# Causal mask of an attention stage: added on VectorE in PSUM in place of a TensorE product with the identity

## The reference

```python
def block(args):
    qb, cb, s0 = args
    s = jnp.einsum('bhqd,bhkd->bhqk', qb, kh).astype(f32) * scale
    s = s + cb[..., None] - c[:, :, None, :]
    q_pos = s0 + jnp.arange(Q_BLOCK, dtype=jnp.int32)
    mask = k_pos[None, :] <= q_pos[:, None]
    p = jax.nn.softmax(jnp.where(mask, s, -jnp.inf), axis=-1)
    return jnp.einsum('bhqk,bhkd->bhqd', p.astype(vh.dtype), vh)
```

## Time and profile before

| | us |
|---|---|
| median of 3 runs | 2705.4 |
| the 3 runs | 2704.35, 2705.4, 2709.52 |
| the profiled execution | 2702.63 |
| its span, first to last instruction | 2700.8 |
| PE busy in it | 2632.7 (97%) |
| DVE busy | 1499.2 (56%) |
| ACT busy | 1115.2 (41%) |
| POOL busy | 882.5 (33%) |
| mean granted clock of TensorE | 0.989 |

### The profile page before, as it was taken

How to read it: one execution, slowest core, us unless ns; L and a number is a source line. 1 busy time by engine, 2 the same in 40 slices (tenths; PEclk the granted TensorE clock), 3 DMA queues, 4 the chain that set the end, 5 groups by cost and what they waited for, 6 DMA issues and landing times.

```text
span 2700.8 us, 34562 instructions
## 1 busy us (share of the span) xinstructions
PE 2632.7 (97%) x13990; PEld 2201.0 (81%) x13990; DVE 1499.2 (56%) x1688; ACT 1115.2 (41%) x1301; POOL 882.5 (33%) x201
## 2 busy tenths in 40 slices
PE   7989889999899999999999999999999999999998
PEld 6866778888798988888888888898988888888887
DVE  3674646999763383354674346734473364645435
ACT  4364535778534442334332223434433343422222
POOL 2211020000132344444444443433343454344444
PEclk9999988999999999999999999999999999999999
DMA  3330024999221373223233333321662232333332
GB/s 135 118 134 17 1 100 165 367 372 371 76 94 63 126 290 130 78 101 125 101 108 125 119 116 117 106 79 63 233 220 94 94 117 94 109 117 118 120 129 109
DMA packets 61300, 361.26 MB, mean 134 GB/s; under 512 B 7280, under 2 KB 8176, under 8 KB 26096
## 3 DMA queue, kind: packets, MB, share of 16 engines
q1 hardware_dynamic: 58720, 353.49, 35.7%
q10 hardware_dynamic: 2448, 5.90, 0.6%
HBM read 357.25 MB, written 2.10 MB: 133 GB/s over the span
## 4 chain that ended last, share of the span: by engine, by line
PE 80%; DVE 4%; ACT 1%; issue 1%; ACTq 0%; DVEq 0%
PE pd L270 19%; PE pd L272 19%; PE pd L271 19%; PE pd L291 2%; PE pd L290 2%; PE pd L289 2%; PE pd L2142 2%; PE pd L2144 2%; PE pd L2143 2%; DVE sb_y_lo L1874 2%; DVE sb_h_lo L543 1%; PE pd L2169 1%; PE pd L2171 1%; PE pd L2170 1%; PE pd L2099 1%
## 5 line engine op out<-in xcount | busy, mean ns | idle before, releaser
L224 POOL TENSOR_TENSOR sb_w_lo<-sb_raw,sb_w_hi 128x2048 fp32r<-128x2048 f32 x181 | 845.4, 4671 | 1715.7 <-ACT sb_w_hi L215 1715.7
L270 PE MATMUL pd<-sb_h_hi,sb_w_hi 128*128 128x512 f32 x1600 | 635.7, 397 | 11.4 <-DVE sb_h_lo L543 5.1
L272 PE MATMUL pd<-sb_h_hi,sb_w_lo 128*128 128x512 f32 x1600 | 625.2, 391 | 0.0
L271 PE MATMUL pd<-sb_h_lo,sb_w_hi 128*128 128x512 f32 x1600 | 625.0, 391 | 0.0
L215 ACT CAST sb_w_hi<-sb_raw 128x2048 fp32r<-128x2048 f32 x185 | 353.6, 1912 | 349.8 <-PE pd L272 324.3
L270 PE MATMUL pd<-sb_y_hi,sb_w_hi 128*128 128x512 f32 x960 | 376.2, 392 | 8.0 <-DVE sb_y_lo L1885 3.9
L272 PE MATMUL pd<-sb_y_hi,sb_w_lo 128*128 128x512 f32 x960 | 374.1, 390 | 0.0
L271 PE MATMUL pd<-sb_y_lo,sb_w_hi 128*128 128x512 f32 x960 | 374.1, 390 | 0.0
L270 PEld LDWEIGHTS pd<-sb_h_hi,sb_w_hi 128*128 128x128 f32 x1600 | 301.6, 189 | 80.5 <-issue 6.8
L272 PEld LDWEIGHTS pd<-sb_h_hi,sb_w_lo 128*128 128x128 f32 x1600 | 301.5, 188 | 63.8
L271 PEld LDWEIGHTS pd<-sb_h_lo,sb_w_hi 128*128 128x128 f32 x1600 | 301.8, 189 | 62.4 <-issue 1.9
(11 more groups left out here) (568 smaller groups left out, 3837.4 us busy)
## 6 DMA issues: line engine op xcount, KB each, us to landing
sb_raw<-in_slabs SPq DMA_DIRECT2D x190, 1024.0 KB, 4.7
sb_moe_raw<-in_moe SPq DMA_DIRECT2D x56, 1024.0 KB, 5.0
sb_raw<-in_moe SPq DMA_DIRECT2D x28, 1024.0 KB, 4.8
sb_QK<-in_ada SPq DMA_DIRECT2D x32, 512.0 KB, 5.2
sb_V<-in_ada SPq DMA_DIRECT2D x32, 512.0 KB, 5.5
sb_M<-in_ada SPq DMA_DIRECT2D x16, 512.0 KB, 3.6
sb_Y<-in_ada SPq DMA_DIRECT2D x16, 512.0 KB, 5.5
sb_MG<-in_ada SPq DMA_DIRECT2D x16, 512.0 KB, 5.6
```

The costliest lines, as they stand in the source:

```text
L224: pool.tensor_tensor(w_lo[j][:], raw[j][:], w_hi[j][:].bitcast(F32), ALU.subtract).then_inc(w_lo_ready[j], 1)
L270: pe.matmul(out, w_hi[j][:, cols], hi[:, k], start=(k == 0), stop=False)
L271: pe.matmul(out, w_hi[j][:, cols], lo[:, k], start=False, stop=False)
L272: last = pe.matmul(out, w_lo[j][:, cols], hi[:, k], start=False, stop=(k == KT - 1))
```

## The change

The second product of scores(n) is taken out, and the first one closes the accumulation and raises sc_done. VectorE, once sc_done is there, adds maskneg to the last 128 columns of the same PSUM bank, in place, waits for that to end (through v) and then takes the maximum as before.

```diff
-                          start=True, stop=False)
-                pe.matmul(out[:, keys - P:keys], ident[:], maskneg, start=False, stop=True).then_inc(sc_done, 1)
+                          start=True, stop=True).then_inc(sc_done, 1)
...
                     dve.wait_ge(sc_done, n + 1)
                     if n >= 4:
                         dve.wait_ge(sc_exp, n - 3)
+                    last = pd[n % 2][:, keys - P:keys]
+                    v(dve.tensor_tensor(last, last, maskneg, ALU.add))
                     v(dve.tensor_reduce(small[:, 32 + n % 4:33 + n % 4], pd[n % 2][:, 0:keys], AX.X, ALU.max,
                                         negate=True), sc_max, n + 1)
```

## The result

| | before | changed |
|---|---|---|
| median | 2705.3 us (20 runs) | 2717.5 us (20 runs) |
| profiled execution | 2702.63 us | 2722.2 us |
| its span | 2700.8 us | 2720.4 us |
| its granted clock | 0.989 | 0.979 |

The changed kernel takes 1.0048 times the time of the kernel before (95% interval 1.0034 to 1.0061), by this ratio 13 us more. The forecast was 2709.0 us (+3.6) with a range up to 2715. Two of the 20 runs of the changed kernel lie far outside the rest, at 3768.9 us (mean clock 0.65) and 13337.6 us (1.00); why is not known, the ratio and all that follows leave them out, and the median of the other 18 is 2717.0 us.

What follows compares the result with a forecast made beforehand. The prediction took a loop through TensorE, VectorE and ScalarE to bound the score units. Additions of 6.27 us, less 1.53 us of products and 1.16 us of idle time, gave +3.6 us on 2705.4: 2709.0 us, range 2702 to 2715.

Steps and rivals of the forecast that it cites:

- one more stretch at the half clock: Rival, slower: wider TensorE gaps bring one or two more 3 us half-clock stretches, 2710.5 to 2712 us; chance 0.10.
- The price of the addition: Each VectorE mask addition in the score units: 0.29 us plus 0.04 wait, 0.33 us (bounds 0.20 and 0.73).
- The expensive write to PSUM: Rival, slower: VectorE's addition writing to PSUM takes 0.42 us plus 0.04, +6.1 us, 2711.5 us; chance 0.12.
- Units 4 to 7: Score units with VectorE's queue unbroken: TensorE's saving brings nothing, four additions cost 4 x 0.33 = +1.32 us.
- latency sum: Over the score units: 19 additions, 6.27 us, less 1.53 us of products and 1.16 us of idle time: +3.6 us.
- units that I gave to VectorE's queue or to ScalarE: Score units such as 4 to 7 (VectorE) or 8, 9, 22, 23 (ScalarE), where TensorE's saving was counted as nothing.
- Units 0 to 3 at nothing: Beside the recurrence: product hidden beneath VectorE's work, addition fits in 0.62 us idle; cost nothing, without cover 1.3 us.
- The exponential's wait: Sign in the score units: ScalarE's wait for the maximum grows from 36.4 us, by about 0.1 us a unit or more.
- VectorE's wait for TensorE: Sign in the score units: the maximum's wait for the mask product, 13.2 us, passes to the addition and shrinks.
- TensorE decides everywhere: Rival, faster: additions hide in VectorE's idle time, each unit gives back its product, 7.0 us, 2698.4 us; chance 0.06.
- every addition counts: Rival, slower: all 32 additions on the path, TensorE's saving never, 10.6 us, 2716.0 us; chance 0.12.
- The slower sign: Whole kernel slower by over 0.2%, above 2710.8 us; chance 0.32, summed from rivals and the forecast's own tail.

Runs made afterwards that it cites:

- neither: The kernel before without the mask product on TensorE and without the addition on VectorE, so with no causal mask: 2707.7 us, ratio 1.0027.
- again: The changed kernel run once more, unaltered: 2718.3 us (5 runs), ratio 1.0068 to the kernel before.
- the kernel with the four kept products: The changed kernel with the mask product kept in units 0 to 3 and filler products ahead of the transposes from unit 4 on: 2708.1 us, ratio 1.0028.
- the early mask product: The kernel before with the mask product issued first in its accumulation, one iteration sooner: ratio 1.0004; with the 12 fillers added 2701.5 us, ratio 0.9999.

## Why the prediction was wrong

**The part that failed is the rival that I called one more stretch at the half clock.** I gave it a chance of 0.10 and one or two stretches of 3 us, 1.5 us each. The changed kernel's mean clock is 0.0061 below that of the kernel before. Over 2717 us this is about 33 us more at the half clock, where the rival had three or six. Its price, 0.5 us for each, was not far off: the changed kernel's two profiles gave 0.36 us, and the slopes of 1.78 to 2.55 us for 0.001 of the mean clock make 0.0061 worth 11 to 16 us, against a measured loss of 13. So the mechanism was on the list, and its size was wrong by a factor of five or more. Two steps led there. I priced the removed product by its time on the path alone, so a product beneath a wait had the price zero; "neither" shows that removing all 32 of them, with nothing added, makes the kernel slower by 0.27% while its level falls by 3.4 us. And I took the two half-clock stretches of one profile as fixed, where the runs of the kernel before spread from 0.984 to 0.991 of mean clock. The page that I cited beside that rival (the Trainium skill, TensorE: Matmul & The Clock Gate, on oscillation) names this mechanism, gaps in the matmul stream that bring the 1.2 GHz level back, and the traces agree: behind a stretch in which PE was busy 0.30 of 3 us the clock fell to 0.62, and with that stretch filled it stayed at 1.00.

**The price of the addition was right.** 300 ns measured, 285 to 290 taken; with its wait 0.33 us (the rows below: 0.34 from start to start). The expensive write to PSUM, a rival with 0.12, did not happen. Of the two estimates that I had from the Trainium skill (VectorE: DVE Perf Modes, TRN2 errata), 0.291 us is 3% short of the measured 0.300, and 0.258 us 14%. In the changed kernel's units 4 and 5, at the full clock:

```profile
292.09 0.30 DVE L1676 TENSOR_TENSOR pd<-pd,sb_c 128x128 f32<-128x128 f32 x1
...
292.43 0.69 DVE L1677 TENSOR_REDUCE sb_small<-pd 128x1 f32<-128x512 f32 x1
...
295.60 0.30 DVE L1676 TENSOR_TENSOR pd<-pd,sb_c 128x128 f32<-128x128 f32 x1
...
304.93 0.69 ACT L1370 ACTIVATE sb_H<-pd,sb_small 128x512 f32<-128x512 f32 x1 [3.03 <-DVE sb_small L1677]
```

**Units 4 to 7: right.** From the maximum of unit 4 (292.43) to the exponential of unit 7 (304.93) it took 12.50 us; before it was 286.75 to 298.25, 11.50. Three additions lie between, 3 x 0.33 = 1.0. The stretch ran at the full clock.

**The rest of the latency sum: the right sign of each term, in total too large or just right.** It had +5.1 us for the additions and -1.5 for the products. The levels give +4.5 and -3.4, the lines at 0.988 +4.5 and -2.8. The removed product was worth about twice what I gave it: I counted 6 of the 32 on the path, and 2.8 to 3.4 us at 0.22 is 13 to 15. In units that I gave to VectorE's queue or to ScalarE, TensorE's saving seems to have arrived all the same; which units these are was not resolved. For the whole change the levels give zero (2699.8 and 2699.0 against 2699.7), the lines +2.2 us at 0.988, the profiles about 1.5. The predicted +3.6 us is at the upper end of this and is neither confirmed nor refuted.

**Units 0 to 3 at nothing: right by latency.** The kernel with only these four units changed has the level 2699.5 and a ratio of 1.0008 that can't be told from 1.

**What the prediction said it would show.** The exponential's wait grew, as said. VectorE's wait for TensorE grew in the first profile (17.9 against 13.2 us) and shrank, as said, in that of "again" (9.5 us), which had less half clock; so the growth was the sign that time was lost by TensorE's clock. The transposes I had wrongly put 0.22 us behind their old place relative to the score passes: without the product they come sooner, in unit 5 0.92 us after the score product's start ("again", 286.82 to 287.74) and not 1.13 (287.06 to 288.19). Of the gap after the last maximum I had said that it stays as it was: it was 10.8 us before (353.71 to 364.50) and is 11.1 us (370.03 to 381.16).

**The other rivals.** That TensorE decides everywhere (faster) and that every addition counts were both refuted by the comparisons at an equal clock, which lie between them. The slower sign had 0.32 in all; the mechanism that decided had only 0.05 of that, half of its own 0.10.

**What stays open.** Shown is that removing the product lowers the granted clock, that keeping it holds the clock, and that the loss of time follows the clock. Not settled is why nearly as many products elsewhere (30 fillers) win back only about half of it (0.9849 and 0.9853 against 0.9878); the kernel with the four kept products is too near to both to tell. Also open is why units 0 to 3 run at the half clock in some executions of the changed kernel (the first profile) and not in others ("again").

## What to carry to other kernels

In a stage where TensorE waits for other engines all the time, price a removed TensorE operation twice: by its time on the path, and by what the granted clock does afterwards; the second can be several times the first and of the other sign. Before trusting a latency sum of a few microseconds, set each run's time against its mean granted clock, and compare kernels at an equal clock: that splits latency from clock with runs that one has anyway. Do it at a clock that both kernels reached: the slope of time over clock was 2.55 us for one of these kernels and 1.78 for the other, and a common slope hides a few microseconds. Where PE stands idle for microseconds, useless products into a free bank raise the clock; whether they pay is less sure. 12 of them made this kernel 0.19% faster (0.05 to 0.32%) in one set of runs, and in another, together with the early mask product, they gained nothing.

## What was not expected of the hardware

- The mean granted clock of the same kernel differs between executions (0.984 to 0.991 over 112 runs of the kernel before on three chips, with about the same spread on each), and explains nearly all of its scatter of 19 us: 2.55 us for 0.001, with 0.8 us left.
- The clock answered unevenly to TensorE's work in this stage: -0.0043 without the 32 small products (0.22 us each), +0.0006 with twice as many (standard errors 0.0012 and 0.0004).
- VectorE adding in place in PSUM took 300 ns for 128x128, only 15 ns more than the same addition from PSUM to SBUF.
